# Expert weights fetched in 2 MB transfers with 16 KB contiguous per partition, and the feature order this gives

## The chip, the cores and the metric

The kernel runs on one core of one Trainium2 chip. The metric is the device time of one execution in microseconds (us); shorter is better. An engine is one of TensorE (PE in the profile), VectorE (DVE), ScalarE (ACT), GpSimd (POOL) and SyncE (SP). Weights come from HBM through the core's 16 DMA engines; in the stage looked at here all of them are issued by SP, in program order.

## The reference

A hybrid layer (a mixer with a short convolution, stick-breaking attention and forgetting attention, then a mixture of experts) is followed by two further layers (mixers and SwiGLU feed-forward), on 256 tokens of 1024 features, in float32. What matters here is the mixture of experts with 32 experts, top 4, and an expert width of 1024:

```python
def moe_ffn(h, router_w, router_b, w_mlp1, b_mlp1, w_mlp2, b_mlp2):
    xt = h.reshape(b * s, d)
    logits = (xt @ router_w + router_b).astype(jnp.float32)
    top_vals, top_idx = lax.top_k(logits, TOP_K)
    top_w = jax.nn.softmax(top_vals, axis=-1)
    ...
    def expert_step(acc, params):
        w1, b1, w2, b2, gate_e = params
        u = xt @ w1 + b1
        glu = jnp.minimum(u[:, ::2], SWIGLU_LIMIT)
        lin = jnp.clip(u[:, 1::2], -SWIGLU_LIMIT, SWIGLU_LIMIT)
        a = glu * jax.nn.sigmoid(SWIGLU_ALPHA * glu) * (lin + 1)
        out = a @ w2 + b2
        return acc + gate_e[:, None] * out.astype(jnp.float32), None
```

One expert has a `w_mlp1` of 1024 x 2048 floats (8 MB) and a `w_mlp2` of 1024 x 1024 floats (4 MB); 32 of them are 384 MB (402.7 million bytes), and each is read once.

## The kernel before

**The ring.** All large weights go through a ring of 14 slots in SBUF. A slot is one unit of 2048 floats per partition, 1 MB over 128 partitions. `ring_order` lists the units in the order in which they are fetched and gives each its slot, its semaphore count and the unit that was in the slot before. SP walks the same order: `fill` waits until the slot's former unit is used up (`emptied`), and issues one DMA. A semaphore for each slot tells the reader that the unit has landed (`landed`).

**Units of an expert.** `("w1", e, k)`, k = 0 to 7, holds rows 128k to 128k+127 of `w_mlp1[e]`, one row of 8 KB on each partition. `("w2", e, k)`, k = 0 to 3, holds rows 256k to 256k+255 of `w_mlp2[e]` as two rows of 4 KB on each partition, row 128c+p on partition p. The order is w1(e, 2..7), w1(e+1, 0..1), w2(e, 0..3), and so on; the last expert takes its w2 units as 0, 2, 1, 3. So the fetch list is 256 units of w1 and 128 units of w2, each 1 MB. The expert units follow 20 units of earlier weights (`ada`, `out`, `scale2`, `gate2`), which are fetched in stages before.

**PE in the expert stage.** Tokens are gathered for groups of four experts with up to 64 places each (`gather`, `CAP`). For an expert, PE works through w1(e, 0..7) with `mlp1` (L884, eight matmul records for a unit), then after the activation through w2(e, 0..3) with `mlp2` (L902, eight records for a unit). In between it does the scatter of the previous expert (`back`, L909), the gather of a later group (L855), the bias (L877) and four transposes of the activations (`mlp2_turn`, L893). w1(e+1, 0) stands between the end of w1(e, 7) and the transposes, and covers the activation chain, which is `glu` on DVE (L1951 to L1960) with a sigmoid on ACT. An expert with over 64 tokens runs further matmuls on the same units (`more_mlp1` L928, `more_mlp2` L941); then its units are used up only after these.

**The last expert.** `last_unit` does w1(31, 7) in two halves at L1037, and `last_second` interleaves the activation and w2 in halves. Its result feeds the scatter `last_back` (L1187) and everything that follows.

**Feature order.** Contraction block k of mlp1 is features 128k to 128k+127 on the partitions. So the tokens' normed activations `HH` (ACT, L2583) and `HL` (DVE, `h_rest` L1854) are in natural order, as are the router weights `rw`, the transposed residual `x_turn` (L801), and the per-feature scale and shift (`a2`, `sh2`, from transposes of `modr` and of the gain rows, L536). In the same way block q of the activated hidden features is natural for w2.

Of the kernel before, what the change touches and what calls it, by code (L numbers as in the profile page):

```python
# [113 lines left out]
def w2_order(e):  # L114

    return (0, 2, 1, 3) if e == NEXP - 1 else (0, 1, 2, 3)


def ring_order():
# [4 lines left out]
    order += [("w1", 0, 0), ("w1", 0, 1)]  # L124
    for e in range(NEXP):
        order += [("w1", e, k) for k in range(2, 8)]
# [13 lines left out]
    for n, name in enumerate(order):  # L140
        if n == first:
            slots, at = [(at + i) % 8 for i in range(8)] + list(range(8, NRING)), 0
# [5 lines left out]
        units[name] = (s, 16 * uses[s], prior[s])  # L148
        prior[s] = name
    return units  # L150


def build(nc, I, out, counts, counting):
    with ExitStack() as ctx:
# [31 lines left out]

        def landed(name):
            s, n, _ = units[name]
            return s_slot[s], n

        def unit(name):
            s = units[name][0]
# [31 lines left out]
        X = v1(o_x, 2048).rearrange("p (t d) -> p t d", t=2)  # L224
        o_rows = al(1024)
# [52 lines left out]
        a1, s1 = sm(8), sm(8)  # L278
# [193 lines left out]
        def emptied(name):  # L472
# [37 lines left out]
        def _(pe):  # L510
# [278 lines left out]
            for cc in range(4):  # L789
                t = pe.matmul(PS[:, 7, 2 * cc:2 * cc + 2], modr[:, 2, cc * 128:(cc + 1) * 128], both, start=True, stop=True)  # L790
# [16 lines left out]
            for cc in range(4):  # L807
                t = pe.transpose(PS[:, 0, cc * 128:(cc + 1) * 128], modr[:, 1, cc * 128:(cc + 1) * 128], ident)
# [111 lines left out]

            def more_bias(e):
                for g in range(4):
                    pe.matmul(PS[32 * g:32 * g + 32, HB[1][0], :], SB1[e % 2][:, g // 2, 0:MORE].bitcast(F32),
                              B1S[:, g % 2 * 512:g % 2 * 512 + 512].bitcast(F32), start=True, stop=False)

            def more_mlp1(u, x, k8):
                for g in range(4):
                    t = pe.matmul(PS[32 * g:32 * g + 32, HB[1][0], :], x[:, k8, :], u[:, g * 512:(g + 1) * 512],  # L928
                                  start=False, stop=k8 == 7)
# [15 lines left out]
            def second_start(e, more_than):  # L945
                n0 = W1B.n
                with pe.If(more_than):
# [4 lines left out]
                    for k8 in (0, 1):  # L952
                        t = more_mlp1(unit(("w1", e, k8)), XGM[e % 2], k8)
# [2205 lines left out]
```

## Time and profile before

| | us |
|---|---|
| median of 3 runs | 1663.6 (1663.06 to 1664.67) |
| span of the profiled execution | 1663.7 |
| before the first expert unit is issued | 0 to 159.7 |
| first expert matmul (L884) | 202.9 |
| last expert matmul (L902) ends | 1156.2 |
| second part (two further layers), to the end | 1168.5 to 1663.7 |

The profile is one execution; its span is within 0.1 us of the median, so that a difference in the span is read as a difference in the time. PE is busy 1538.4 us (92%), DVE 666.6 us, ACT 453.4 us. The queue of SP moves 529.99 MB. Times within the profile are counted from the start of the span. "Who waited" and "idle before" name what ended an idle time last.

### The profile page before, as it was taken

What the parts mean: (1) busy time and instruction counts of PE and PEld (TensorE: products, weight loads), DVE (VectorE), ACT (ScalarE), POOL (GpSimd) and SP (SyncE); (2) the same over time, 40 slices, a digit from 0 to 9 for tenths busy, and PEclk for the clock granted to TensorE, in tenths of its full rate; (3) what the DMA queues carried; (4) which work ended last, traced back from release to release, by engine and by line L of the source; (5) the groups of instructions that cost most, each with busy time, mean ns of one, the idle gap of its engine ahead of it and who ended that gap; (6) DMA issues with size and microseconds to landing.
All of it is one profiled execution on the core that took longest, in us unless ns stands there. A gap on an engine that the chain in (4) does not pass through costs nothing.

```text
span 1663.7 us, 21829 instructions
## 1 busy us (share of the span) xinstructions
PE 1538.4 (92%) x8565; PEld 862.7 (52%) x8565; DVE 666.6 (40%) x956; ACT 453.4 (27%) x752; POOL 99.5 (6%) x114
## 2 busy tenths in 40 slices
PE   5999999999998888999898888887899999999998
PEld 2887633333332323333222322222858998799986
DVE  3576632222323223223221231222876565466654
ACT  3574411111110010111010100001865444354443
POOL 3032000000000000000000000000440000400000
PEclk9999999999999999999999999999899999999999
DMA  9647999999999999999999999999436555455540
GB/s 362 190 159 280 415 415 417 414 418 416 415 417 415 416 417 415 417 415 415 417 415 410 418 410 416 414 415 357 169 126 196 195 180 183 146 190 186 195 152 26
DMA packets 152930, 534.28 MB, mean 321 GB/s; under 512 B 9810, under 2 KB 72937, under 8 KB 117825
## 3 DMA queue, kind: packets, MB, share of 16 engines
q1 hardware_dynamic: 150832, 529.99, 81.5%
q8 instruction: 121, 1.98, 0.5%
q0 software_dynamic: 1936, 1.98, 0.4%
q14 instruction: 41, 0.33, 0.1%
HBM read 530.87 MB, written 1.05 MB: 320 GB/s over the span
## 4 chain that ended last, share of the span: by engine, by line
PE 61%; DMA 19%; DVE 5%; ACT 2%; issue 1%; SPq 0%; DVEq 0%
PE ps L884 19%; DMA ring<-in_w_mlp 19%; PE ps L497 8%; PE ps L499 8%; PE ps L498 8%; PE ps L902 7%; PE ps L909 2%; PE ps L855 2%; PE ps L928 1%; DVE arena L1960 1%; PE ps L1318 1%; DVE arena L1951 1%; DVE arena L1956 1%; PE ps L893 1%; PE ps L1309 1%
## 5 line engine op out<-in xcount | busy, mean ns | idle before, releaser
L884 PE MATMUL ps<-ring,arena 128*64 128x512 f32 x2040 | 490.5, 604 | 23.2 <-DMA ring<-in_w_mlp 23.0
L902 PE MATMUL ps<-ring,arena 128*64 128x512 f32 x1024 | 237.7, 601 | 31.1 <-DMA ring<-in_w_mlp 24.9
L884 PEld LDWEIGHTS ps<-ring,arena 128*64 128x64 f32 x2040 | 127.8, 136 | 265.7 <-issue 191.5
L1479 DVE TENSOR_TENSOR wl<-ring,wh 128x1024 fp32r<-128x1024 f32 x132 | 162.1, 1232 | 136.2 <-ACT wh L2348 136.2
L497 PE MATMUL ps<-hth,wh 128*128 128x256 f32 x704 | 201.3, 286 | 0.8 <-DVE htl L2139 0.8
L498 PE MATMUL ps<-htl,wh 128*128 128x256 f32 x704 | 199.0, 283 | 0.0
L499 PE MATMUL ps<-hth,wl 128*128 128x256 f32 x704 | 198.4, 282 | 0.0
L1944 DVE TENSOR_TENSOR arena<-ps,arena 128x1024 f32<-128x1024 f32 x68 | 83.2, 1224 | 252.5 <-PE ps L909 245.7
L2348 ACT ACTIVATE wh<-ring 128x1024 fp32r<-128x1024 f32 x132 | 139.2, 1059 | 149.2 <-PE ps L499 149.2
L902 PEld LDWEIGHTS ps<-ring,arena 128*64 128x64 f32 x1024 | 71.0, 137 | 191.6 <-issue 117.0
L1965 DVE TENSOR_TENSOR arena<-ps,arena 128x512 f32<-128x512 f32 x34 | 23.5, 691 | 357.8 <-PE ps L902 354.7
L498 PEld LDWEIGHTS ps<-htl,wh 128*128 128x128 f32 x704 | 136.1, 193 | 0.0
L499 PEld LDWEIGHTS ps<-hth,wl 128*128 128x128 f32 x704 | 134.9, 192 | 0.0
L497 PEld LDWEIGHTS ps<-hth,wh 128*128 128x128 f32 x704 | 134.0, 190 | 1.3 <-issue 1.0
L2631 ACT ACTIVATE obh<-arena 128x512 fp32r<-128x512 f32 x30 | 18.9, 630 | 313.5 <-DVE arena L1965 313.5
L2610 ACT ACTIVATE arena<-arena 128x512 f32<-128x512 f32 (+1 forms) x33 | 20.4, 617 | 303.0 <-DVE arena L1951 303.0
L497 PE MATMUL ps<-wh,fth 128*128 128x512 f32 x176 | 69.8, 396 | 0.0
L498 PE MATMUL ps<-wl,fth 128*128 128x512 f32 x176 | 69.6, 395 | 0.0
L499 PE MATMUL ps<-wh,ftl 128*128 128x512 f32 x176 | 69.5, 395 | 0.0
L2591 ACT ACTIVATE arena<-ps,arena 128x256 f32<-128x256 f32 x60 | 30.5, 559 | 121.7 <-PE ps L855 116.6
L2999 POOL MEMSET arena<- 128x1144 f32 x1 | 1.1, 1056 | 1015.3 <-DVE htl L2139 1015.3
L497 PE MATMUL ps<-wp,ht 128*128 128x384 f32 (+1 forms) x128 | 46.4, 362 | 3.7 <-DVE ht L1535 2.3
(439 smaller groups left out, 1830.4 us busy)
## 6 DMA issues: line engine op xcount, KB each, us to landing
ring<-in_w_mlp SPq DMA_DIRECT2D x384, 1024.0 KB, 21.6
ring<-in_w_ada SPq DMA_DIRECT2D x24, 1024.0 KB, 14.4
ring<-in_ffn_w_gate SPq DMA_DIRECT2D x22, 1024.0 KB, 5.2
ring<-in_ffn_w_up SPq DMA_DIRECT2D x22, 1024.0 KB, 5.2
ring<-in_ffn_w_down SPq DMA_DIRECT2D x22, 1024.0 KB, 4.7
ring<-in_w_in SPq DMA_DIRECT2D x10, 768.0 KB, 11.9
ring<-in_w_in_ab SPq DMA_DIRECT2D x6, 1024.0 KB, 13.9
ring<-in_w_out SPq DMA_DIRECT2D x4, 1024.0 KB, 8.2
```

The costliest lines, as they stand in the source:

```text
L497: pe.matmul(o, lh, rh, start=first, stop=False)
L498: pe.matmul(o, lh, rl, start=False, stop=False)
L499: return pe.matmul(o, ll, rh, start=False, stop=last)
L855: t = pe.matmul(PS[:, bank, (k % 2) * 256:(k % 2) * 256 + 256], H[:, i, k * 128:(k + 1) * 128], ST[:, i, :], start=i == 0 and H is HH, sto ...
L884: t = pe.matmul(PS[64 * g:64 * g + 64, HB[hb][ns], :], x[:, k8, :], u[:, f:f + 512], start=False, stop=k8 == 7)
L902: t = pe.matmul(PS[64 * g:64 * g + 64, 3, :], a4[:, kc, 64 * kg:64 * kg + 64], u[:, c, g * 512:(g + 1) * 512], start=k8 == 0, stop=k8 == 7)
L909: t = pe.matmul(PS[:, b + g, :], SGT[k][64 * g:64 * g + 64, i * 128:(i + 1) * 128], O[64 * g:64 * g + 64, :], start=O is OBH[s], stop=O is ...
L1479: dve.tensor_tensor(l, src, h.bitcast(F32), ALU.subtract).then_inc(*V.tick((st, "lo", n)))
L1944: dve.tensor_tensor(x, PS[:, b:b + 2, :], x, ALU.add).then_inc(*tick(name))
L1965: dve.tensor_tensor(OBF, PS[:, bank, :], G2R, ALU.mult).then_inc(*tick(n_f))
L2348: act.activation(h, src, ACT.Copy).then_inc(*S.tick((st, "hi", n)))
L2591: act.activation(XGT[b % 2][:, k, :], PS[:, bank, (k % 2) * 256:(k % 2) * 256 + 256], ACT.Identity, scale=a2[:, k:k + 1], bias=sh2[:, k:k ...
```

## The change

Two neighbouring ring slots hold one 2 MB transfer. `wide` names the units that come so: all of w1, and w2 of all experts but the last. A w1 transfer k (0, 2, 4, 6) takes rows 128k to 128k+255 as `(p c) n -> p (c n)`: partition p gets the two neighbouring rows 2p and 2p+1, 16 KB in one run. A w2 transfer k (0, 2) takes rows 256k to 256k+511 as `(p q) n`: partition p gets rows 4p to 4p+3, also 16 KB in one run. Each such DMA waits for both slots' former units; `unit` and `landed` lead the odd units to the pair's slots and semaphore. There are 128 + 62 such transfers and 4 of 1 MB (w2 of the last expert), 194 in place of 384.

A contraction block of mlp1 is now the even or the odd features of a stretch of 256. What supplies these is rewritten: `HH` and `HL` are each written in two instructions (one for even, one for odd features) in place of one, `x_turn` and the transposes of `modr` read with a step of two, the router's weights are fetched in pairs of rows, and the gain row of the norm is transposed a second time in this order (8 more transposes at the start, one DVE copy, `g2col`). A contraction block of mlp2 is every fourth hidden feature, so `glu` reads PSUM with a step of 8 floats in place of 2 and writes four blocks (`turn=4`); for the last expert it stays as it was. The overflow matmuls of experts with over 64 tokens read their weight columns in groups of four (`quarter`).

```diff
 def w2_order(e):
-    return (0, 2, 1, 3) if e == NEXP - 1 else (0, 1, 2, 3)
+    return (0, 2, 1, 3) if e == NEXP - 1 else (0, 2)
+def wide(name):
+    return name[0] == "w1" or name[0] == "w2" and name[1] < NEXP - 1
...
-            order += [("w1", e + 1, 0), ("w1", e + 1, 1)]
+            order += [("w1", e + 1, 0)]
...
+        before = [prior[s]]
         prior[s] = name
+        if wide(name):
+            t = slots[at % len(slots)]
+            at += 1
+            assert s % 2 == 0 and t == s + 1
+            before.append(prior[t])
+            prior[t] = name
+        units[name] = (s, 16 * uses[s], [b for b in dict.fromkeys(before) if b is not None])
...
             if kind == "w1":
-                return [name, ("w1b", name[1], (0, 0, 1, 1, 2, 2, 2, 2)[name[2]])]
+                return [("w1", name[1], name[2] + 1), ("w1b", name[1], (0, 1, 2, 2)[name[2] // 2])]
             if kind == "w2":
-                return [name, ("w2b", name[1])]
+                return [("w2", name[1], name[2] + wide(name)), ("w2b", name[1])]
...
+            for k in range(8):
+                pe.transpose(PS[:, 1, 64 + k * NROW:64 + (k + 1) * NROW], strided(A[0:NROW, o_rows:o_rows + 1024], k),
+                             CT(C_IE + 128, NROW, 0, NROW))
...
-                    t = pe.transpose(PS[:, b, o:o + 128], X[:, i, k * 128:(k + 1) * 128], ident)
+                    t = pe.transpose(PS[:, b, o:o + 128], strided(X[:, i, :], k), ident)
...
+                for c in range(2):
+                    dve.scalar_tensor_tensor(out=apart(HL[:, i, :], c0, c1)[:, :, c, :], in0=pairs(X[:, i, :], c0, c1)[:, :, c, :],
+                                             scalar=rr[i], in1=apart(HH[:, i, :].bitcast(F32), c0, c1)[:, :, c, :],
+                                             op0=ALU.mult, op1=ALU.subtract).then_inc(*V.tick(("HL", i)))
...
+                if turn:
+                    U = PF[:, 512 * b:512 * (b + nb)].rearrange("p (a q two) -> p q a two", q=turn, two=2)
+                    GO, LO = (w.rearrange("p (q a) -> p q a", q=turn) for w in (G, L))
...
-                act.activation(HH[:, i, :], X[:, i, :], ACT.Copy, scale=rr[i]).then_inc(*S.tick(("HH", i)))
+                for c in range(2):
+                    act.activation(apart(HH[:, i, :], 0, 1024)[:, :, c, :], pairs(X[:, i, :], 0, 1024)[:, :, c, :], ACT.Copy,
+                                   scale=rr[i]).then_inc(*S.tick(("HH", i)))
...
-                sp.dma_start(view(ring[:, s * UNIT:(s + 1) * UNIT]), src).then_inc(s_slot[s], 16)
+                sp.dma_start(view(ring[:, s * UNIT:(s + 1 + wide(name)) * UNIT]), src).then_inc(s_slot[s], 16)
...
+            def w1_rows(e, k):
+                return I["w_mlp1"][0, e][k * 128:k * 128 + 256, :].rearrange("(p c) n -> p (c n)", c=2)
...
+                    if wide(("w2", e, k)):
+                        fill(("w2", e, k), lambda u: u,
+                             I["w_mlp2"][0, e][k * 256:k * 256 + 512, :].rearrange("(p q) n -> p (q n)", q=4))
```

The change regroups work more than it moves it. The place for SP is the start of the expert stage, from w1(0, 0) on. The bracket is what a DMA waits for: `s_pe_front`, `s_dve_oproj`, `s_pe_oproj` and `s_pe_route` are counts of earlier stages, `s_pe_moe` is PE's count of used units, `s_pe_w1b` and `s_pe_w2b` are the counts of the overflow matmuls. SP before:

```order
L3032 DMA ring<-in_w_mlp 128x2048 [waits s_pe_front] x2
L3032 DMA ring<-in_w_mlp 128x2048 [waits s_dve_oproj] x4
L3032 DMA ring<-in_w_mlp 128x2048 [waits s_pe_oproj] x4
L3032 DMA ring<-in_w_mlp 128x2x1024 [waits s_pe_route] x3
L3032 DMA ring<-in_w_mlp 128x2x1024 [waits s_pe_moe]
L3032 DMA ring<-in_w_mlp 128x2048 [waits s_pe_w1b,s_pe_moe] x8
L3032 DMA ring<-in_w_mlp 128x2x1024 [waits s_pe_w1b,s_pe_moe] x2
L3032 DMA ring<-in_w_mlp 128x2x1024 [waits s_pe_w2b,s_pe_moe] x2
```

SP in the changed kernel, at the same place:

```order
L3084 DMA ring<-in_w_mlp 128x4096 [waits s_pe_front]
L3084 DMA ring<-in_w_mlp 128x4096 [waits s_dve_oproj] x2
L3084 DMA ring<-in_w_mlp 128x4096 [waits s_pe_oproj] x2
L3084 DMA ring<-in_w_mlp 128x4096 [waits s_pe_route]
L3084 DMA ring<-in_w_mlp 128x4096 [waits s_pe_moe,s_pe_route]
L3084 DMA ring<-in_w_mlp 128x4096 [waits s_pe_w1b,s_pe_moe] x5
L3084 DMA ring<-in_w_mlp 128x4096 [waits s_pe_w2b,s_pe_moe] x2
```

The twelve issues of an expert, each of 2048 floats per partition, have become six of 4096, each with the waits of both its slots. On PE the only new instructions stand at the start, where the seven gain rows are transposed; before:

```order
L530 MATMUL ps<-arena 128x8
L517 MATMUL ps<-ring,arena 32x512 x24
L536 MATMUL ps<-arena 128x7 x8
L539 MATMUL ps<-arena 128x4
L525 MATMUL ps<-arena 128x128 x16
L517 MATMUL ps<-ring,arena 32x512 x8
```

and in the changed kernel:

```order
L561 MATMUL ps<-arena 128x8
L548 MATMUL ps<-ring,arena 32x512 x24
L567 MATMUL ps<-arena 128x7 x8
L570 MATMUL ps<-arena 128x7 x8
L573 MATMUL ps<-arena 128x4
L556 MATMUL ps<-arena 128x128 x16
L548 MATMUL ps<-ring,arena 32x512 x8
```

Eight transposes (L570) now stand ahead of the one of the four head gains (L573) and of the turning of the first normed activations (L556).

## Rows read from the trace of the kernel before

**Rows 1.** The page: span; PE's busy tenths and the GB/s, 40 slices.
```profile
span 1663.7 us, 21829 instructions
...
PE   5999999999998888999898888887899999999998
...
GB/s 362 190 159 280 415 415 417 414 418 416 415 417 415 416 417 415 417 415 415 417 415 410 418 410 416 414 415 357 169 126 196 195 180 183 146 190 186 195 152 26
```

**Rows 2.** The page: the chain that ended last, by engine; the two expert matmul groups.
```profile
PE 61%; DMA 19%; DVE 5%; ACT 2%; issue 1%; SPq 0%; DVEq 0%
...
L884 PE MATMUL ps<-ring,arena 128*64 128x512 f32 x2040 | 490.5, 604 | 23.2 <-DMA ring<-in_w_mlp 23.0
L902 PE MATMUL ps<-ring,arena 128*64 128x512 f32 x1024 | 237.7, 601 | 31.1 <-DMA ring<-in_w_mlp 24.9
```

**Rows 3.** DMA issues of the expert weights: count, KB each, median us to landing.
```profile
ring<-in_w_mlp SPq DMA_DIRECT2D x384, 1024.0 KB, 21.6
```

**Rows 4.** Windows: length, busy us (instructions) by engine, PE clock, DMA share, GB/s.
```profile
180.00:200.00 20.00, 19.08 (x156) 13.95 (x153) 16.73 (x49) 9.64 (x23) 0.00 (x0) 1.00 1.01 420
204.00:210.00 6.00, 5.91 (x55) 2.50 (x53) 0.74 (x3) 0.60 (x1) 0.00 (x0) 1.00 1.03 410
...
177.00:1154.00 977.00, 903.84 (x4524) 311.41 (x4523) 267.09 (x394) 110.49 (x218) 0.00 (x0) 1.00 1.01 414
```

**Rows 5.** The ring unit w1(1, 1), issued alone in its window at 183.5 us.
```profile
DMA to landing us min/median/max: 18.7/18.7/18.7
```

**Rows 6.** The ring unit w2(0, 3), issued at 202.3 us.
```profile
DMA to landing us min/median/max: 10.1/10.1/10.1
```

**Rows 7.** The ring unit w1(2, 1), issued at 224.0 us.
```profile
DMA to landing us min/median/max: 8.2/8.2/8.2
```

**Rows 8.** PE: w2 of experts 0, 2 and 6 in the chain of waits.
```profile
229.52 6.87 PE ps L902 x32
...
281.82 6.87 PE ps L902 x32
...
405.22 6.87 PE ps L902 x32
```

**Rows 9.** PE: the overflow matmuls of mlp1, by line (32 for an expert).
```profile
L928 PE MATMUL ps<-ring,arena x128: 592/592/617, 339.9 to 696.8; 128*32 128x512 f32 x128
```

**Rows 10.** PE in order of time, late: start, us, line, idle before and releaser.
```profile
1121.61 1.94 PE L902 MATMUL ps<-ring,arena 128*64 128x512 f32 x8
...
1141.67 1.94 PE L884 MATMUL ps<-ring,arena 128*64 128x512 f32 x8 [0.53 <-DMA ring<-in_w_mlp]
...
1144.27 1.94 PE L1037 MATMUL ps<-ring,arena 128*64 128x512 f32 x8
```

**Rows 11.** A unit issued into an empty queue, at 123.2 us.
```profile
DMA to landing us min/median/max: 4.9/4.9/4.9
```

**Rows 12.** The ring unit w1(1, 2), issued at 208.0 us.
```profile
DMA to landing us min/median/max: 6.9/6.9/6.9
```

**Rows 13.** SP in order of time: the issue of w2(1, 1), by itself.
```profile
229.56 0.38 SPq L3032 DMA_DIRECT2D ring<-in_w_mlp  x1
```

**Rows 14.** A ring unit issued at 384.0 us, after the second overflowing expert.
```profile
DMA to landing us min/median/max: 9.3/9.3/9.3
```

**Rows 15.** PE in order of time, early: the transposes of the gain rows and what follows.
```profile
25.76 0.70 PE L536 MATMUL ps<-arena 7*128 7x7 f32 x5
...
26.71 3.68 PE L525 MATMUL ps<-arena 128*128 128x128 f32 x16
30.31 2.12 PE L517 MATMUL ps<-ring,arena 128*32 128x512 f32 x16
```

**Rows 16.** DVE: reading PSUM with a step of two (L1951), and contiguously (L1965).
```profile
L1951 DVE TENSOR_SCALAR arena<-ps x35: 414/690/693, 224.1 to 1147.3; 128x512 f32<-128x512 f32 x31, 128x256 f32<-128x256 f32 x4
...
L1965 DVE TENSOR_TENSOR arena<-ps,arena 128x512 f32<-128x512 f32 x34 | 23.5, 691 | 357.8 <-PE ps L902 354.7
```

**Rows 17.** DVE and ACT in order of time: the writing of HL and HH.
```profile
191.98 0.74 DVE L1854 SCALAR_TENSOR_TENSOR hl<-arena,hh 128x512 fp32r<-128x512 f32 x1
192.85 0.41 DVE L1862 SCALAR_TENSOR_TENSOR arena<-ps,arena 128x32 f32<-128x32 f32 x2
...
190.28 2.18 ACT L2583 ACTIVATE hh<-arena 128x1024 fp32r<-128x1024 f32 x2
```

More of the change, by code:

```diff
@@ L123, in ring_order @@
     order += [("ada", 1, k) for k in range(8)] + [("out", kk) for kk in range(4)] + [(w, k) for w in ("scale2", "gate2") for k in range(4)]
-    order += [("w1", 0, 0), ("w1", 0, 1)]
+    order += [("w1", 0, 0)]
     for e in range(NEXP):
-        order += [("w1", e, k) for k in range(2, 8)]
+        order += [("w1", e, k) for k in (2, 4, 6)]
         if e + 1 < NEXP:
-            order += [("w1", e + 1, 0), ("w1", e + 1, 1)]
+            order += [("w1", e + 1, 0)]
         order += [("w2", e, k) for k in w2_order(e)]
@@ L185, in build, with held @@
         units = ring_order()
+        def held(name):
+            c = name[2] % 2 if wide(name) else 0
+            return (name[0], name[1], name[2] - c) if c else name, c
         def landed(name):
-            s, n, _ = units[name]
+            s, n, _ = units[held(name)[0]]
             return s_slot[s], n
         def unit(name):
-            s = units[name][0]
+            of, c = held(name)
+            s = units[of][0] + c
             return ring[:, s * UNIT:(s + 1) * UNIT]
@@ L224, in build, with pairs, apart, strided @@
         X = v1(o_x, 2048).rearrange("p (t d) -> p t d", t=2)
+        def pairs(rows, lo, hi):
+            return rows[:, lo:hi].rearrange("p (m q c) -> p m c q", q=128, c=2)
+        def apart(rows, lo, hi):
+            return rows[:, lo:hi].rearrange("p (m c q) -> p m c q", q=128, c=2)
+        def strided(rows, k):
+            return rows[:, 256 * (k // 2) + k % 2:256 * (k // 2) + 256:2]
         o_rows = al(1024)
@@ L789, in _ @@
             for cc in range(4):
-                t = pe.matmul(PS[:, 7, 2 * cc:2 * cc + 2], modr[:, 2, cc * 128:(cc + 1) * 128], both, start=True, stop=True)
+                t = pe.matmul(PS[:, 7, 2 * cc:2 * cc + 2], strided(modr[:, 2, :], cc), both, start=True, stop=True)
             t.then_inc(*P.tick("scale2 turned"))
@@ L919, in again_gather, with quarter @@
                 slot_gate(lambda i: ST2[:, i, :], 260, e).then_inc(*Q.tick(name))
+            def quarter(e, rows, h):
+                if e == NEXP - 1:
+                    return rows[:, 512 * h:512 * h + 512]
+                return rows.rearrange("p (a h f) -> p h a f", h=2, f=4)[:, h, :, :]
             def more_bias(e):
@@ L952, in second_start @@
                     for k8 in (0, 1):
-                        t = more_mlp1(unit(("w1", e, k8)), XGM[e % 2], k8)
+                        t = more_mlp1(e, unit(("w1", e, k8)), XGM[e % 2], k8)
                     t.then_inc(*W1B.tick(("w1b", e, 0)))
@@ L1154, in _ @@
                         for n in range(4, 8):
-                            t = more_mlp1(unit(("w1", e, n)), XGM[e % 2], n)
+                            t = more_mlp1(e, unit(("w1", e, n)), XGM[e % 2], n)
                         t.then_inc(*W1B.tick(("w1b", e, 2)))
@@ L1885, in _ @@
             dve.tensor_tensor(gt, gt, eq, ALU.add).then_inc(*V.tick("chosen"))
-            h_rest(0, slice(512, 1024))
+            h_rest(0, 512, 1024)
             dve.wait_ge(*done("places"))
@@ L1907, in _ @@
             dve.tensor_copy(most, cmax).then_inc(*V.tick("cnt"))
-            h_rest(1, slice(0, 1024))
+            h_rest(1, 0, 1024)
             dve.wait_ge(*done("pos turned"))
@@ L2051, in _ @@
                 if more:
-                    glu(V, 0, b0, 2, gsl[:, e:e + 1], ("w1", e, 7), ("glu in", e), ("hid", e), ("sigmoid", e), ("glu", e))
+                    glu(V, 0, b0, 2, gsl[:, e:e + 1], ("w1", e, 7), ("glu in", e), ("hid", e), ("sigmoid", e), ("glu", e),
+                        turn=4)
                 else:
@@ L2060, in _ @@
                     glu(V2, 1, HB[1][0], 1, gsl2[:, e % 2:e % 2 + 1], ("w1b", e, 2), ("glu in2", e), ("hid2", e),
-                        ("sigmoid2", e), ("glu2", e))
+                        ("sigmoid2", e), ("glu2", e), turn=2 * more)
                 with dve.Else():
@@ L3027, in fill @@
             def fill(name, view, src):
-                s, _, prior = units[name]
-                if prior is not None:
+                s, _, before = units[name]
+                for prior in before:
                     for step in emptied(prior):
                         sp.wait_ge(*done(step))
-                sp.dma_start(view(ring[:, s * UNIT:(s + 1) * UNIT]), src).then_inc(s_slot[s], 16)
+                sp.dma_start(view(ring[:, s * UNIT:(s + 1 + wide(name)) * UNIT]), src).then_inc(s_slot[s], 16)
             def fill_rows(name, w, r0, nk, c0, ncol):
@@ L3091, in _ @@
                         sp.wait_ge(*done(("back", NEXP - 1, 1)))
-                        for k in range(8):
-                            sp.dma_start(ring[:, k * UNIT:(k + 1) * UNIT],
-                                         I["w_mlp1"][0, e][k * 128:(k + 1) * 128, :]).then_inc(s_load["again"], 16)
+                        for k in range(0, 8, 2):
+                            sp.dma_start(ring[:, k * UNIT:(k + 2) * UNIT], w1_rows(e, k)).then_inc(s_load["again"], 16)
                         for k in range(4):
```

58 lines of the change are left out of this document (30 added, 28 removed).

## The prediction

> **What bounds the kernel now.** First the page by slices: from slice 5 to 27 the DMA engines move 410 to 418 GB/s without a break while PE is busy 0.8 to 0.9 of the time [rows 1]. So for the 977 us from 177 to 1154 us, in which the 402.7 million bytes of expert weights land, the queue is never empty: its share is 1.01 and its mean 414 GB/s [rows 4]. Second, the chain of waits gives PE 61% and DMA only 19% [rows 2]; that is a matter of where the chain is read. PE starts late against a full ring and works unhindered at first: mlp2 of experts 0 and 2 starts at 229.5 and 281.8 us, 26.15 us per expert, and from 281.8 to 405.2 us it takes four experts 123.4 us, 18.8 us more than 4 x 26.15, for two overflowing experts, 9.4 us each [rows 8]. Four experts overflow (128 records of L928, 32 for each) [rows 9]. PE alone would so come to mlp2 of expert 30 at 229.5 + 30 x 26.15 + 4 x 9.4 = 1052 us; it comes at 1121.6 us, and behind it waits for a unit to land [rows 10]. The weights' rate sets the end of this stage, and PE has about 70 us to spare. All after it hangs on this end and moves with it.
>
> **The rate, by length of run.** The landing times of four ring units show it at steady load. w1(1, 1), issued at 183.5, lands at 202.2 us; w2(0, 3), four w2 units later, at 202.3 + 10.1 = 212.4; w1(2, 1), eight w1 units later, at 224.0 + 8.2 = 232.2 [rows 5 to 7]. A w2 unit (runs of 4 KB) takes 10.2 / 4 = 2.55 us, a w1 unit (runs of 8 KB) 19.8 / 8 = 2.48 us. The windows agree: 420 GB/s (2.50 us) with w1 alone, 410 (2.56 us) with w2 alone [rows 4]. So 128 more runs of half the length cost a megabyte 0.06 to 0.07 us. Runs of 16 KB leave out 64 more of them from w1 and 192 from w2: 2.48 - 0.035 = 2.445 us and 2.55 - 0.105 = 2.445 us, or 4.89 us for a transfer of 2 MB.
> - w1: 256 units x 0.035 = 9.0 us; w2: 31 experts x 4 units x 0.105 = 13.0 us. Together -22.0 us; with 0.06 in place of 0.07 it is -19. The completions halve too; no row prices one, and I give them 1 us of the rounding: **-23 us**. As a bound from below zero gain: w1 none, if 16 KB runs are served as two of 8 KB, and then w2 124 x 0.07 = 8.7 us.
> - The 977 us hold 256 x 2.48 + 124 x 2.55 + 4 x 2.55 = 961 us of such transfer time; the other 16 us are irregular delays, and I let them stand.
>
> **Half as many transfers** cost or give little by themselves: a unit takes 21.6 us from issue to landing [rows 3] and one lands every 2.5 us, so some eight are in flight and fixed times of one are behind the others. The Trainium skill ("DMA: Bandwidth & Descriptors", Anatomy of one DMA) fits one DMA alone as 2.0 us plus bytes at 436 GB/s. Paid each time, 190 fewer transfers would give 380 us; the rows above speak against that, since a unit would then take 4.4 us and not 2.5.
>
> **Slots in pairs.** A transfer waits for the second slot of its pair, so its first megabyte is issued later. Is the queue then ever dry? A unit issued into an empty queue takes 4.9 us [rows 11], 2.4 more than 2.48; a 2 MB transfer then 7.3 us. Where the queue is thinnest:
> - w1(1, 2), issued at 208.0, lands 6.9 us later, at 214.9 [rows 12]. The pair of it and the next would land at 214.9 + 2.5 - 0.8 (five w1 pairs x 0.07 and two w2 pairs x 0.21 gained by then) = 216.6, and the fourth pair after that, w2(1, 0..1), at 236.2. Its second slot is free at 229.6 us [rows 13], so it can't land before 236.9: +0.7 us. After it PE frees twelve units in 26.15 us and the queue needs 29.3, so it fills up.
> - w2(6, 2), issued at 384.0 after two overflowing experts, lands at 393.3 [rows 14]. The pair would land at 393.3 + 2.5 - 4.3 (gained by then: 23 / 977 of 214 us, less the 0.7) = 391.5; its second slot is free some 0.4 us after the first, and it can't land before 384.4 + 7.3 = 391.7: +0.2 us.
> Together **+1 us**; 0 if the 2.4 us overlap in part, 4 us if PE is later by one or two at both places.
>
> **The last pair.** PE waits for w1(31, 6) at 1141.67 us and then goes from it to w1(31, 7) at 1144.27 without a wait [rows 10]; the latter lands 2.5 us after the former. In one transfer both land with the later, PE does two units behind it, and all after is PE, DVE and ACT in series: **+2.5 us**. The w2 units of this expert stay single and land while PE works.
>
> **The start.** The 8 transposes and the next one take from 25.8 to 26.7 us and PE is in a row of work up to 32.4 us [rows 15]; 8 more add **+0.8 us** to everything behind, the DMA stage too.
>
> **The rewritten order.** HL in halves of 256: DVE is free at 192.7 us, and the top-8 path starts at 192.85 [rows 17]; one more instruction puts about 0.1 to 0.3 us on it. HH, x_turn and modr with a step of two: nothing for the step by my reading, since DVE reads PSUM at a step of two in 690 ns and contiguously in 691 [rows 16]. All this lies behind a queue that is full by then; it only moves the first matmul, and through it the thin places: **+0.3 us**. The same two rows are the nearest for `glu` at a step of 8. If this took twice as long, 1.4 us per expert, PE would need 27.6 us per expert against 29.3 of DMA, and nothing is lost; the last expert keeps the old step. The operands of all mlp1 and mlp2 matmuls but those of the four overflowing experts stay contiguous.
>
> **Sum**, against the profiled span of 1663.7 us, 0.1 over the median: -23 + 1 + 2.5 + 0.8 + 0.3 = -18.4, so a span of 1645.3 and a median of **1645.2 us**. PE's reserve of 70 us falls to about 50. Its waits get longer and fewer, up to 1.5 us before a w2 pair; they are 0.5 us now [rows 10].
>
> **The rivals.**
> - *16 KB runs are served in pieces of 8 KB or less.* For it: no run of 16 KB of weights is in this trace. Against it: 4 and 8 KB are each one run. Only w2 gains, -8.7, and the costs of 4.6 us stay: 1659.5 us. Chance 0.12.
> - *The longer run gains more*: the 16 us of irregular delays are partly of the same kind and halve: 1645.2 - 8 = 1637.2 us. Chance 0.08.
> - *The queue runs dry oftener.* With seven pairs in place of 14 units PE holds up to 4 MB at a time; if each of the 31 experts loses 0.4 us, that is +12: 1657.2 us. Against it: 21.6 us in flight [rows 3] are four pairs and more. Chance 0.08.
> - *Slower: the 16 DMA engines, whose reads then start twice or four times as far apart in HBM, get in each other's way.* Place: every expert transfer from 177 us on. It decides from 4.98 us for 2 MB: the pairs take 128 x 4.96 + 62 x 5.10 = 951.1 us now, and (951.1 - 4.6) / 190 = 4.98; above it the change loses. At the 410 GB/s of w2 [rows 4] a pair takes 5.11 us, 190 x 5.11 - 951.1 = +19.8, and with the costs of 4.6 us the time is 1688.0 us. Against it: the step from 4 to 8 KB made the rate higher. Chance 0.12. The Trainium skill ("DMA: Bandwidth & Descriptors", Latency and other measured facts) has such a loss for copies of 16 KiB rows with a pitch of 512 KiB and more; here the rows lie next to each other, and no run here shows such a pitch.
>
> **Numbers.** Forecast 1645.2 us, chance 0.60; its own range is 1641 to 1652 (above: -19 in place of -23, and 4 us of dry queue in place of 1; below: no dry queue and no loss in the rewritten order, and 3 us more from the rate). The range from 1637 to 1660 takes in the first three rivals, the outer ones at its ends, and leaves out the slower one and what lies beyond the ends, less than 2 in 10. A measurement tells about 0.2% (3.3 us) from no change. Faster: 0.60 + 0.08 + 0.08 + half of 0.12 = 0.82; same 0.06; slower 0.12.
>
> **What would show it.** The rate in the stage at 428 GB/s within 2, landings of 2 MB 4.9 us apart, runs of 16 KB counted as one packet each; the last w1 matmuls at about 1126 us, without a wait between them; queue share 1.0 throughout but for a microsecond near 232 and 387 us; the first transposes 0.8 us later. It is wrong if the rate stays at 420 or below, if SP issues pairs when the queue is dry, or if PE stops waiting for weights.

## The result and the profile after

The changed kernel takes 1647.5 us (median of 4 runs, 1646.7 to 1649.7) against 1663.3 us (4 runs, 1662.6 to 1664.7) for the kernel before beside it: 0.9903 of its time, 95% interval 0.9892 to 0.9915, or 15.9 us less. The prediction was 1645.2 us, with 1637 to 1660. In the later experiments the same kernel was timed again beside the one before: 0.9892 (0.9873 to 0.9911), 18.7 us less. The profiled execution has a span of 1644.7 us, and it is the quickest of its four. An execution takes up to 2.4 us more than its span (1646.7 against 1644.7 us here). So the profiled one of before, with a span of 1663.7 us, can only be its slowest (1664.7 us), although its span lies near the median of the times. The two spans differ by 19.0 us.

The page of the changed kernel: span, PE's busy tenths and GB/s in 40 slices, the two expert matmul groups, the expert DMAs. It answers [rows 1 to 3].

```profile
span 1644.7 us, 21485 instructions
...
PE   5999999999999889999988898886999999999998
...
GB/s 362 197 159 278 425 395 428 426 424 419 426 426 426 426 427 425 428 425 426 426 425 426 427 426 425 427 425 331 138 102 218 182 192 190 128 200 192 185 154 26
...
L918 PE MATMUL ps<-ring,arena 128*64 128x512 f32 x2040 | 486.9, 603 | 30.2 <-DMA ring<-in_w_mlp 27.5
...
L936 PE MATMUL ps<-ring,arena 128*64 128x512 f32 x1024 | 230.1, 595 | 19.9 <-DMA ring<-in_w_mlp 14.2
...
ring<-in_w_mlp SPq DMA_DIRECT2D x190, 2048.0 KB, 26.7
```

Where 410 to 418 GB/s stood from slice 6 on (counted from 0), there are now 424 to 428 in nearly all of them. Slice 5 (206 to 247 us) fell instead, from 415 to 395: that is the first thin place of the queue. Ahead of the two expert groups PE is idle for 30.2 and 19.9 us, where it was 23.2 and 31.1 [rows 2]: the sum is smaller. The waits for a landing are fewer and longer, 40 of up to 1.46 us in this stage in place of 87 of mostly 0.5 to 0.6 us (by the idle times in the two traces). The windows give the same by stretch; they answer [rows 4] (columns as there).

```profile
180.00:200.00 20.00, 19.08 (x160) 14.38 (x162) 17.18 (x55) 10.95 (x26) 0.00 (x0) 1.00 1.00 424
200.00:250.00 50.00, 49.41 (x255) 17.26 (x255) 16.05 (x25) 7.03 (x14) 0.00 (x0) 1.00 1.00 402
250.00:350.00 100.00, 97.18 (x517) 36.42 (x515) 27.23 (x41) 10.76 (x21) 0.00 (x0) 1.00 1.01 426
...
900.00:1000.00 100.00, 87.30 (x400) 29.75 (x401) 23.12 (x30) 10.18 (x20) 0.00 (x0) 1.00 1.01 426
177.00:1135.00 958.00, 890.00 (x4507) 315.17 (x4507) 266.88 (x396) 111.06 (x220) 0.00 (x0) 1.00 1.00 422
```

PE in order of time, at the end of the expert stage, answers [rows 10]: start, length, line, then the idle time before and its releaser.

```profile
1105.45 3.65 PE L936 MATMUL ps<-ring,arena 128*64 128x512 f32 x16 [0.51 <-DMA ring<-in_w_mlp]
1110.37 3.65 PE L936 MATMUL ps<-ring,arena 128*64 128x512 f32 x16 [1.26 <-DMA ring<-in_w_mlp]
1115.27 3.65 PE L918 MATMUL ps<-ring,arena 128*64 128x512 f32 x16 [1.25 <-DMA ring<-in_w_mlp]
1120.16 1.94 PE L918 MATMUL ps<-ring,arena 128*64 128x512 f32 x8 [1.24 <-DMA ring<-in_w_mlp]
...
1125.06 1.94 PE L918 MATMUL ps<-ring,arena 128*64 128x512 f32 x8 [0.44 <-DMA ring<-in_w_mlp]
...
1127.60 1.94 PE L1077 MATMUL ps<-ring,arena 128*64 128x512 f32 x8
...
1143.78 1.22 PE L1227 MATMUL ps<-obh,sgt 64*128 64x512 f32 x4 [4.33 <-issue]
```

Here PE waits for every pair and is released every 4.89 or 4.90 us (1110.37, 1115.27, 1120.16, 1125.06): that is one transfer of 2 MB. L1227 is the scatter of the last expert (`last_back`, L1187 before), on which all that follows depends.

**A sum from landings.** In this document the stage is cut by three events: R, the landing of the last `gate2` unit, which is the last transfer ahead of the expert weights; L, the landing of the last expert unit; and S, the start of the last scatter. A landing is counted when the slowest of the 16 DMA engines has ended. The times come from the landing records of each trace and count from the start of the span, as in the rows. (Some landing and issue times in the expectations below are 0.2 us later than by this count.)

| | R | R to L | L to S | S to end | span |
|---|---|---|---|---|---|
| before | 177.3 | 976.9 | 8.6 | 501.0 | 1663.7 |
| after | 176.0 | 959.0 | 8.7 | 500.9 | 1644.7 |
| difference | -1.3 | -17.8 | +0.1 | -0.1 | -19.0 |

The median distances of landings are 2.488 us for a w1 unit and 2.545 us for a w2 unit before (256 and 128 of them: 962.7 us), and 4.894 us for a pair after, with 2.51 for the four single units (939.9 us). What is left of R to L is called irregular here: 14.2 us before, 19.1 us after. So the rate gave 22.8 us, and 5.0 us came back in the same stage.

### The profile page after: what moved, and what is told of

Same layout as the page of the kernel before. It is cut to its first block, busy times and chain, and to the rows that moved or that the text cites. A ratio compares the mean times of both kernels' runs of the same rounds, so it can differ in the third digit from the quotient of the medians.

```text
span 1644.7 us, 21485 instructions
## 1 busy us (share of the span) xinstructions
PE 1524.7 (93%) x8573; PEld 864.9 (53%) x8573; DVE 667.4 (41%) x960; ACT 453.8 (28%) x754; POOL 99.7 (6%) x114
## 4 chain that ended last, share of the span: by engine, by line
PE 33%; DMA 17%; DVE 3%; ACT 2%; issue 1%; DVEq 0%
DMA ring<-in_w_mlp 17%; PE ps L528 8%; PE ps L530 8%; PE ps L529 8%; PE ps L918 4%; PE ps L936 3%; PE ps L1358 1%; PE ps L1349 1%; DVE ps L2234 1%; DVE wm L1519 1%; PE ps L1486 0%; PE ps L1502 0%; ACT arena L2809 0%; PE ps L943 0%; ACT hth L2771 0%
## 5 line engine op out<-in xcount | busy, mean ns | idle before, releaser
L918 PE MATMUL ps<-ring,arena 128*64 128x512 f32 x2040 | 486.9, 603 | 30.2 <-DMA ring<-in_w_mlp 27.5
L918 PEld LDWEIGHTS ps<-ring,arena 128*64 128x64 f32 x2040 | 129.6, 136 | 268.8 <-issue 205.4
L936 PE MATMUL ps<-ring,arena 128*64 128x512 f32 x1024 | 230.1, 595 | 19.9 <-DMA ring<-in_w_mlp 14.2
L936 PEld LDWEIGHTS ps<-ring,arena 128*64 128x64 f32 x1024 | 74.7, 137 | 168.9 <-issue 134.5
## 6 DMA issues: line engine op xcount, KB each, us to landing
ring<-in_w_ada SPq DMA_DIRECT2D x24, 1024.0 KB, 14.2
```

The source lines that it names most:

```text
L918: t = pe.matmul(PS[64 * g:64 * g + 64, HB[hb][ns], :], x[:, k8, :], u[:, f:f + 512], start=False, stop=k8 == 7)
L936: t = pe.matmul(PS[64 * g:64 * g + 64, 3, :], a4[:, kc, 64 * kg:64 * kg + 64], u[:, c, g * 512:(g + 1) * 512], start=k8 == 0, stop=k8 == 7)
```

## The experiments

All of them are timed beside the kernel before (median 1665.6 us in the first set, 1665.4 in the second, 1664.8 in the third); a ratio is to that, and its brackets are the 95% interval.

**Length of run or size of transfer?** `e1_2mb_short` is the kernel before (rows and features in their old order) with the two neighbouring units in one transfer of 2 MB:

```diff
-                    fill_rows(("w1", e, k), I["w_mlp1"][0, e], k * 128, 1, 0, 2048)
+                    fill_rows(("w1", e, k), I["w_mlp1"][0, e], k * 128, 2, 0, 2048)
-                    fill_rows(("w2", e, k), I["w_mlp2"][0, e], k * 256, 2, 0, 1024)
+                    fill_rows(("w2", e, k), I["w_mlp2"][0, e], k * 256, 2 + 2 * wide(("w2", e, k)), 0, 1024)
```

> The kernel before with its natural feature order, but with the 190 transfers of 2 MB in paired slots; the runs stay 8 KB (w1) and 4 KB (w2). Theory (the length of a run sets the rate): landings 4.96 us apart for a w1 pair and 5.10 for a w2 pair, no gain, and the costs of the pairs stay: +2.5 us for the last pair and 1 to 2.5 us of dry queue, 1667 us, ratio 1.002. Rival (the size of the transfer, or their number, sets the rate): 4.89 us apart, about 1648 us, ratio 0.991.

Measured: 1668.0 us, 1.0019 (1.0009 to 1.0029). Its windows and DMA issues:

```profile
177.00:1150.00 973.00, 893.89 (x4486) 312.24 (x4478) 264.29 (x388) 109.20 (x215) 0.00 (x0) 0.99 1.01 414
...
ring<-in_w_mlp SPq DMA_DIRECT2D x190, 2048.0 KB, 25.9
```

The same 190 transfers, and 414 GB/s as before. Pairs land 4.97 (w1) and 5.08 us (w2) apart, twice 2.49 and 2.54. Larger and fewer transfers give nothing. R to L is 980.1 us in place of 976.9, of which 18.4 are irregular: nearly as much as in the changed kernel (19.1), with the old runs. So most of the 5.0 us that came back is a cost of the pairs, and not of the longer run.

`e2_w2_8k` keeps single units of 1 MB and only gives w2 runs of 8 KB (`(p q) n -> p (q n)` with q=2, and `glu` at a step of 4):

> The kernel before with its 384 transfers of 1 MB in single slots; only w2 (of 31 experts) comes with two neighbouring rows on a partition, runs of 8 KB in place of 4 KB, and the activation is written in that order. Theory: a w2 unit takes 2.48 us in place of 2.55, 124 x 0.07 = 8.7 us less, nothing else changes: 1654.6 us, ratio 0.995. Rival (size or number of transfers): no gain, 1663.3 us.

Measured: 1657.2 us, 0.9958 (0.9941 to 0.9975), 8.4 us less.

```profile
177.00:1140.00 963.00, 895.88 (x4496) 309.41 (x4496) 266.34 (x393) 110.17 (x217) 0.00 (x0) 1.00 1.01 418
```

The landings of w2 units are now 2.486 us apart, as those of w1. The rate goes by the run: 2.545 us per megabyte at 4 KB, 2.486 at 8 KB, 2.447 at 16 KB.

**Short transfers with long runs.** `e3_half_partitions` is the changed kernel with each 2 MB as two transfers, one for each half of the partitions:

```diff
-                sp.dma_start(view(ring[:, s * UNIT:(s + 1 + wide(name)) * UNIT]), src).then_inc(s_slot[s], 16)
+                    for h in range(2):
+                        sp.dma_start(u[64 * h:64 * h + 64, :], src[64 * h:64 * h + 64, :]).then_inc(s_slot[s], 16)
```

> The changed kernel with each 2 MB transfer issued as two of 1 MB, one for partitions 0 to 63 and one for 64 to 127, both on the pair's semaphore; runs stay 16 KB, the number of transfers is again 384. Theory: the rate stays 2.445 us per MB and the time that of the changed kernel within 1.5 us: 1647.5 us, ratio 0.990. Rival (size or number of transfers): the rate falls back to 2.48 us per MB or below, 1663 us or more, ratio 1.000.

Measured: 2253 to 2315 us in six executions; the three quickest (2253, 2260 and 2269 us) give 1.3605 (1.357 to 1.364). Neither theory had this. The profile is of one of the three longer ones (2305.5 us).

```profile
177.00:1700.00 1523.00, 1025.20 (x4260) 332.38 (x4260) 249.62 (x371) 106.68 (x210) 0.00 (x0) 0.86 1.01 247
...
GB/s 350 143 255 231 220 228 223 229 279 289 324 334 287 291 232 229 243 231 228 228 221 221 219 219 218 219 227 234 301 334 305 201 109 215 189 190 156 183 183 55
...
ring<-in_w_mlp SPq DMA_DIRECT2D x384, 1024.0 KB, 46.6
```

The DMA share is full (1.01), at 247 GB/s. This run mixes two things, the smaller transfer and the half of the partitions, so the third set took them apart. `e12_even_odd` splits the same 2 MB into even and odd partitions:

```diff
-                        sp.dma_start(u[64 * h:64 * h + 64, :], src[64 * h:64 * h + 64, :]).then_inc(s_slot[s], 16)
+                        sp.dma_start(u[h:128:2, :], src[h:128:2, :]).then_inc(s_slot[s], 16)
```

> The changed kernel, each 2 MB again as two transfers of 1 MB with runs of 16 KB, but on the even and the odd partitions in place of the lower and the upper 64. Theory (length of the run sets the rate, and the collapse with halves of the partitions came from the halves, which leave each transfer only part of the way into SBUF): 2 MB land every 4.9 us, 426 GB/s, 1646.7 us within 2. Rival (twice the number of transfers, or 64 runs in one, costs by itself): every 2 MB takes over 5.1 us and the time is over 1690 us; if it is all of the collapse, some 2280 us.

Measured: 1646.9 us, 0.9894 (0.9878 to 0.9909), the time of the changed kernel.

```profile
177.00:1130.00 953.00, 888.61 (x4490) 313.62 (x4488) 264.53 (x390) 109.84 (x217) 0.00 (x0) 1.00 1.00 423
...
ring<-in_w_mlp SPq DMA_DIRECT2D x384, 1024.0 KB, 23.8
```

384 transfers of 1 MB, all but four with runs of 16 KB, are as quick as 194 of which 190 have 2 MB. With some transfers always in flight, size and number make no difference here; the run does. The collapse belongs to the halves. The Trainium skill ("SBUF — State Buffer", Door 1: The DMA port swizzle) says that partitions 0 to 63 are reached by eight of the 16 ports, 64 to 127 by the other eight, and gives some 218 GB/s for eight; even and odd partitions each lie on all 16. Most slices of this stage in the run with halves stand at 218 to 231 GB/s, so the trace agrees for them; why it came to 280 to 334 in some stretches isn't shown.

**The dry queue.** In the changed kernel the pairs issued at 206.7 to 228.3 us land 2.5 us later in all than the rate allows. `e5_thin_single` fetches twelve units there singly:

```diff
+def alone(name):
+    return name in [("w1", 1, k) for k in range(2, 8)] + [("w1", 2, 0), ("w1", 2, 1)] + [("w2", 1, k) for k in range(4)]
 def wide(name):
-    return name[0] == "w1" or name[0] == "w2" and name[1] < NEXP - 1
+    return (name[0] == "w1" or name[0] == "w2" and name[1] < NEXP - 1) and not alone(name)
```

The second set timed it together with the changed kernel itself:

> The changed kernel itself, so that the runs beside it can be set against it on the same chip. Both theories expect 1647.5 us within 1.5, 0.990 of the kernel before, ring start to last expert unit 959 us.

> The changed kernel, but the twelve units w1(1, 2) to w1(2, 1) and w2(1, 0) to w2(1, 3) come as single 1 MB transfers of 8 KB runs. In the changed kernel the transfers issued at 206.9, 211.9, 217.8, 222.9 and 228.5 us land 0.92, 0.14, 1.34, 0.09 and 0.02 us later than the rate allows: 2.5 us in all. Theory (SP holds a pair back until its second slot is free, and the queue is dry for this time): the single transfers are issued 1 to 2.5 us earlier, the 2.5 us go, and twelve times 0.035 us for shorter runs come back: 2.1 us less than the changed kernel, 1645.4 us, and ring start to last expert unit 957 us. Rival (a page's width of irregular delays that would come anyway): 0.4 us more than the changed kernel, 1647.9 us, 959.4 us.

Measured: 1646.7 us (0.9892) for the changed kernel, 1649.6 us, 0.9907 (0.9890 to 0.9924), with single units. The edit didn't do what it says: a single transfer still waited for both halves of the pair that had been in its place, so the first ones were issued 31.1 us after R, where the pair was at 30.7. From R to the end this run is the longest of the single ones (1470.7 us, table below). `e9_thin_halves` mends this: each slot waits for its own half.

```diff
-            prior[t] = name
+            prior[t] = (name[0], name[1], name[2] + 1)
...
-                return [("w1", name[1], name[2] + wide(name)), ("w1b", name[1], (0, 1, 2, 2)[name[2] // 2])]
+                return [name, ("w1b", name[1], (0, 1, 2, 2)[name[2] // 2])]
```

> The changed kernel with the same twelve units as single 1 MB transfers as in the run before (w1(1, 2) to w1(2, 1), w2(1, 0) to w2(1, 3)), but each now waits only for the half that was in its own slot; in the run before a single transfer still waited for both halves of the pair that had been in its place, so its first ones were issued no earlier (31.1 us after the last gate2 unit had landed, 30.7 in the changed kernel). Theory (a dry queue costs 2.5 us at this place since pairs are held back): the first of each two is issued some 2 us earlier, the 27th and 28th megabyte of expert weights land 2 us earlier counted from the last gate2 unit, and the time is 2.1 us less, 1644.6 us against 1646.7. Rival (the queue would be as dry with single transfers, since PE frees units no faster): landings and time as in the changed kernel, within 0.5 and 1.5 us.

Measured: 1648.8 us (1645.6 to 1651.1), 0.9908 (0.9893 to 0.9923). No gain, yet the place itself did get better: from the second pair on, the first half is issued 1.7 to 2.9 us earlier counted from R. Its windows at the two thin places of the prediction:

```profile
200.00:250.00 50.00, 49.40 (x257) 17.34 (x251) 16.00 (x25) 6.92 (x13) 0.00 (x0) 1.00 1.00 414
380.00:395.00 15.00, 14.60 (x85) 5.02 (x79) 6.34 (x8) 2.48 (x5) 0.00 (x0) 1.00 0.97 387
```

and the changed kernel in the second of them:

```profile
380.00:395.00 15.00, 14.60 (x85) 5.02 (x79) 6.23 (x7) 2.45 (x5) 0.00 (x0) 1.00 0.99 407
```

The first place rose from 402 to 414 GB/s, and the second fell from 407 to 387. By landings: after 26 MB of expert weights the irregular time is 3.9 us in the changed kernel and 1.2 us with the mended singles; after 88 MB it is 5.5 us in both, and at L 19.1 and 19.2 us. The reason stands in PE. The pair w2(6, 2) waits for slots that PE frees after two overflowing experts: it is issued at 382.9 us in the changed kernel and at 383.1 here, and lands 9.0 us later in both, at 391.9 and 392.1 us. Whatever the queue gained before is waited for here. So single transfers at the first place don't take these 2.5 us out of R to L.

**The last pair.** `e4_last_single` takes w1(31, 6) and w1(31, 7) singly, by the same `alone`:

> The changed kernel, but the last two units of w1, (31, 6) and (31, 7), are fetched as two transfers of 1 MB with runs of 8 KB, so that PE can start on the first 2.5 us before the second lands. Theory (the last pair costs one unit's landing): 2.4 us less than the changed kernel, 1645.1 us, ratio 0.989, and PE waits between the two units or not at all. Rival (the end is set by the w2 units that land after it): no change, 1647.5 us.

Measured: 1648.8 us (1645.0 to 1651.5), 0.9905 (0.9885 to 0.9925). `e6_both` joins it with the first (faulty) singles:

> The former kernel and also w1(31, 6) and w1(31, 7) as single 1 MB transfers. Theory, if both costs are real and nothing takes their place: -2.1 for the dry queue and -2.2 for the last pair, 1643.2 us. Rival, which the run with the last pair alone made single speaks for (0.9905 of the kernel before, where the changed kernel has 0.9903): the 2.2 us are taken back ahead of the scatter of the last expert, where PE stands still behind nothing but its own instruction stream (6.59 us in the kernel before, 4.33 us in the changed one); then only the dry queue counts, 1645.4 us. If neither counts, 1647.5 to 1648 us.

Measured: 1647.9 us, 0.9903 (0.9884 to 0.9921). In both w1(31, 7) began only 0.65 us earlier against the wait before it, since w1(31, 5) comes late in a pair as well. So `e11_last_six` takes six units singly, with the mended waits:

> The changed kernel with w1(31, 2) to w1(31, 7) as six single transfers that wait for their own slot only. With only the last two single, w1(31, 7) began 6.8 us after the last wait for an earlier pair in place of 7.4, since PE was still busy with w1(31, 5), which had come late in a pair itself. Theory (a pair makes PE late by one unit's work, and one single pair at the end can't make up for it): w1(31, 7) begins within 0.3 us of its own landing, 2.3 us earlier against the landing of the last w2 unit than in the changed kernel, and the time is 2 us less, 1644.7 us. Rival (the time is taken back ahead of the scatter of the last expert by PE's own instruction stream): w1(31, 7) is as early, the idle time ahead of the scatter grows from 4.2 to 6.5 us, and the time stays at 1646.7.

Measured: 1648.7 us (1645.5 to 1651.2), 0.9905 (0.9891 to 0.9919). PE in order of time:

```profile
1122.02 1.94 PE L928 MATMUL ps<-ring,arena 128*64 128x512 f32 x8 [0.58 <-DMA ring<-in_w_mlp]
...
1124.55 1.94 PE L1087 MATMUL ps<-ring,arena 128*64 128x512 f32 x8
...
1131.05 5.38 PE L946 MATMUL ps<-ring,arena 128*64 128x512 f32 x24
...
1143.06 1.22 PE L1237 MATMUL ps<-obh,sgt 64*128 64x512 f32 x4 [6.63 <-issue]
```

w1(31, 7) (L1087 here) begins 3.05 us earlier than in the changed kernel and PE's expert work ends at 1136.4 in place of 1139.5 us, while L is 0.6 us earlier. The scatter (L1237) begins after 6.63 us of idle time in place of 4.33: it gains 0.7 us, of which 0.6 come from L. The rival holds, with the figure it gave (6.5). Both edits together, `e10_thin_and_last` (the count in the text on record is wrong, it has 181 pairs):

> Both edits in one kernel: eighteen single transfers, 176 pairs less three and six. Theory: both costs go, 1642.6 us. Rivals: only one goes, 1644.6 us; none goes, 1647 us (18 x 0.035 = 0.6 us for the shorter runs stays).

Measured: 1650.1 us (1646.2 to 1651.0), 0.9905 (0.9890 to 0.9920). Neither goes.

The times of one kernel spread over up to 6.5 us here. In the profiles most of the spread comes from the start (below: R lies between 175.4 and 179.2 us). So 2 us can't be read from these medians. From R to the end the profiles are closer, and say the same:

| | after | after again (e8) | e4 | e5 | e6 | e9 | e10 | e11 | e12 | before |
|---|---|---|---|---|---|---|---|---|---|---|
| R to end, us | 1468.6 | 1467.7 | 1468.4 | 1470.7 | 1468.2 | 1468.0 | 1469.1 | 1468.8 | 1468.9 | 1486.4 |

None of the six edits of this kind (e4, e5, e6, e9, e10, e11) is better than the better of the two profiles of the changed kernel, which differ by 0.9 us; 2 to 4 us were expected. No version that beats it was found.

**The irregular delays.** Before the change the landings come evenly but for ten places where one is 1.1 to 1.5 us late, 82 to 97 us apart (261.2, 343.0, 429.7, ... 1056.5 us). Every eighth 16 KB packet of the instruction queue (q8 on the page) starts 2.3 to 4.5 us ahead of one of them, at 256.7, 340.0 and 426.8 us for the first three. The changed kernel has eleven in its first profile, again each behind an eighth packet; in its second one (e8) there are 20 places late by 0.3 to 1.2 us from 242 us on, and the irregular time is much the same (18.4 us in place of 19.1). So the size of one delay isn't fixed. At the same time the last DMA engine falls behind the first: it lands its part of a unit 2.1 us after it at the start and 11.2 us at L (15.7 after the change, 14.5 in e8). `e7_more_fetches` adds instructions on GpSimd and nothing else:

```diff
+            for e in range(1, NEXP - 1):
+                for _ in range(257):
+                    pool.wait_ge(*done(("w1", e, 7)))
```

> The changed kernel, with 257 more waits on GpSimd for each of experts 1 to 30, each for something long done: they fill about 30 more 16 KB pieces of instruction code, which go through the same 16 DMA engines as the weights, and nothing else waits for them. Theory (irregular delays are instruction fetches: every eighth one meets the engine that is last with the weights and costs it 1.45 us): three to four more such delays, the last expert unit lands 4.4 to 5.8 us later, and the time is 1652 to 1653.5 us. Rival (the delays have another cause, and GpSimd's waits are beside the path): no change, 1647.5 us within 1.5.

Measured: 1651.9 us (1649.4 to 1653.6), 0.9920 (0.9902 to 0.9939), 5.2 us more than the changed kernel beside it. R to L is 964.0 us in place of 958.6, 5.4 more. The instruction queues from 180 to 1130 us, first of the changed kernel, then of this one:

```profile
q8 instruction: 86, 1.41, 0.6%
q14 instruction: 21, 0.17, 0.0%
```

```profile
q14 instruction: 51, 0.42, 0.1%
```

The new packets come through q14 and have 8 KB, so the expected 16 KB was wrong. The form of the delays was wrong too: not three or four more of 1.45 us, but many small ones. Behind 702.8 us, where the first of the new packets starts, 19 landings are late by 0.45 to 0.96 us, 13.0 us together; in the changed kernel beside it there are nine, 5.8 us together. The cost was as expected: thirty packets, 0.25 MB or 0.6 us at 426 GB/s, cost 5.4 us. The last DMA engine ends 19.8 us behind the first at L, in place of 14.5: 5.3 us more, about the same amount. This fits code fetches being paid for in the time of the slowest DMA engine. Which engine a packet goes to is not in the traces, and so why only some of them count stays open.

## Why the prediction was right, point by point

**What bounds the stage: right.** The last waits are some 1.25 us, in place of 0.5 (the longest is 1.46, predicted up to 1.5), and the work behind the stage moved with L.

**The rate: right**, in size and in cause. -22.8 us against -23, 4.894 us for a pair against 4.89, and 426 GB/s in undisturbed windows against 428. The prediction gave the completions 1 us of its rounding. No row priced them, and e12 shows next to nothing: with twice the number of transfers 2 MB still land 4.895 us apart. The rival in which 16 KB is served in pieces falls by these rows; the trace has each such run as one packet of 16384 bytes. The rival with engines in each other's way falls too: in e12 the runs of one transfer even start 32 KB apart in HBM in place of 16 KB, at the same rate.

**The queue runs dry: mis-sized.** The step "+0.7 us" for the first place was 2.5 us. It took one late transfer, at 229.6 us, and priced an issue into an empty queue at 7.3 us. In fact each of the five pairs issued between 206.7 and 228.3 us came into a queue with one or two others in it, and two of them were late: one by 0.9 us, one by 2.8 us, of which 1.45 are counted as one of the irregular delays and 1.3 as dry queue. The second place, "+0.2 us", cost nothing in the changed kernel, because the first had already taken more than its share. The two were added in the prediction; e9 shows that they aren't a sum: mending the first one opens the second, and the moment when PE frees the slots of w2(6, 2), 383 us, decides. A landing of 391.7 us was given as the earliest there, and it is 391.9.

**The last pair: right in itself, wrong on the path.** The pair made PE late by 2.4 us: PE's last expert matmul ends 4.4 us after L (1139.46 against 1135.06), where it was 2.0 (1156.16 against 1154.18). But "all after is PE, DVE and ACT in series" was the failed step. Ahead of the scatter PE stood still for 6.59 us before and for 4.33 now, both put down to nothing but its own instruction stream (`issue` in the row), and nearly all of the 2.4 us went into this. L to S is 8.6 and 8.7 us. The prediction had not looked at this wait, though the kernel before shows it in its row of PE in order of time:

```profile
1162.75 1.22 PE L1187 MATMUL ps<-obh,sgt 64*128 64x512 f32 x4 [6.59 <-issue]
```

It isn't the scatter's data: its first operand (`obh`, from ACT) was ready 5.2 us ahead of it before and 2.9 us after the change, the second (`obl`, from DVE) 4.5 and 2.2 us ahead. What it waited for is argued, and not shown by an edit. In the program PE passes a branch here (`pe.If(over > LIMIT)`), and in the trace two 16 KB instruction packets pass on q8; the second starts 4.6 us after L in both kernels and in e11, and lasts 2.2 us. In the 13 profiles without e3 the scatter begins 1.7 to 1.9 us after this packet has ended, wherever that falls: 4.8 us after L in e7, 6.1 to 6.5 us in e9, e6 and e4, 6.7 to 6.9 us in eight, 8.5 us in e8. L to S goes with it: 6.6 us, 7.9 to 8.3, 8.5 to 8.8, 10.3. PE's last expert matmul ends 2.0 to 6.0 us after L in the same profiles, and the first operand is ready 0.8 to 5.2 us ahead of the scatter. No run moved this packet by itself.

**The start: right, and hidden by something larger.** The eight transposes cost 0.6 us: the next group begins at 27.31 us against 26.71 [rows 15].

```profile
25.75 0.68 PE L567 MATMUL ps<-arena 7*128 7x7 f32 x8
26.29 0.73 PE L570 MATMUL ps<-arena 7*128 7x7 f32 x5
...
27.31 1.97 PE L556 MATMUL ps<-arena 128*128 128x128 f32 x16
```

Yet R is 1.3 us earlier. The 16 transposes behind (L556, L525 before) took 3.68 us before and 1.97 here, with a granted clock of 1.00 in both. This isn't of the change: in e10, with the same instructions, they took 3.67.

```profile
27.23 3.67 PE L566 MATMUL ps<-arena 128*128 128x128 f32 x16
```

In six of the twelve profiles of the experiments and the changed kernel (e3 left out) it was 3.5 to 3.7 us, in the other six 1.97. Where they took 1.97 us, R is at 174.8 and 175.5 us with the old start (e1, e2) and at 175.4 to 176.0 with the new one (after, e9, e11, e12), 0.6 us more in the mean. Where they took 3.5 us or more, it is 177.3 (before) against 177.5 to 179.2, 178.3 in the mean, 0.9 more. So +0.8 fits, and the profile of before, which the sum was made against, happened to be one in which they took 3.68 us. It also goes some way to tell why the profiled spans differ by 19.0 us and the medians by 15.9 and 18.7.

**The rewritten order: right that it costs little.** The top-8 path begins at 191.59 us in place of 192.85, and the first expert matmul at 201.5 in place of 202.8 (not 202.9, as the table ahead has it). Both are 1.3 us earlier, as R is: of the +0.3 us nothing shows. DVE reads PSUM at a step of eight in 692 ns and contiguously in 691:

```profile
L2013 DVE TENSOR_TENSOR arena<-ps,arena 128x512 f32<-128x512 f32 x34 | 23.5, 691 | 339.6 <-PE ps L936 336.4 <-PE ps L981 3.2
...
L2001 DVE TENSOR_SCALAR arena<-ps 128x512 f32<-128x512 f32 x31 | 21.4, 692 | 18.9 <-PE ps L918 18.9
```

HH takes 2.71 us in place of 2.18, HL's pieces 0.87 in place of 0.74 [rows 17].

**The irregular 16 us: not left as they were.** They measure 14.2 us before, and after the change 16.6 us (with one delay more) besides the 2.5 of the dry queue. The rival in which they halve falls: they are 14.7 us in e2 and 18.4 in e1, so they go by the pairs and not by the run.

**The sum as it came out:** -22.8 (rate) + 2.5 (dry) + 2.5 (an eleventh delay and small ones) + 0.8 (start, over many profiles) + 0 (last pair) = -17.0, against -18.4 in the prediction and -15.9 and -18.7 measured. It came out so near in part by luck, because the misses went to different sides: the dry queue 1.5 and the delays 2.5 us too low, the last pair 2.5 and the rewritten order 0.3 too high.

## What to carry to other kernels

Where a stage is bound by a full DMA queue, read the distance of landings for each length of run and multiply; the number and the size of transfers drop out while several are in flight, as long as each covers partitions in both halves. Price a thin place of the queue together with the later ones: where the computing engine decides when slots come free, what was gained or lost before is evened out. And before a delay at the end of a stage is counted, look whether the next engine stands idle behind it on its own account.

## What was not expected of the hardware

- Transfers of 1 MB with runs of 16 KB, issued for partitions 0 to 63 and 64 to 127 in turn, move 247 GB/s; the same for even and odd partitions 423, all at a full DMA share.
- Fetching code takes DMA time where it hurts: 30 packets of 8 KB cost 5.4 us, and in the kernel before each eighth 16 KB packet is followed by a landing 1.1 to 1.5 us late. By the end of the stage the last DMA engine is 11.2 us behind the first before the change, 14.5 and 15.7 after it, and 19.8 with the 30 packets more.
- The last scatter begins 1.7 to 1.9 us after the end of a 16 KB instruction packet in 13 profiles, with PE idle for 2.2 to 6.8 us ahead of it.
- The same 16 transposes near 27 us take 1.97 us in some executions and 3.5 to 3.7 in others, at a granted clock of 1.00 in both, and R differs by 2.2 us (old start) and 2.6 us (new start) in the mean between the two. What sets their pace isn't shown.
